# Ending two stages by token halves, with VectorE alone adding to x

## The reference

```python
y = memory_cross_attention(h, mem_n, w_mem_q, w_mem_kv, w_mem_o)  # ends in o @ w_mem_o, 1024 x 1024
x = x + rmsnorm(y, norm_mem_post)                                 # "mempost"
h = rmsnorm(x, norm_ffn_pre)                                      # "ffn"
y = conv_gated_ffn(h, w_up, ffn_dw, ffn_dw_b, w_down)             # ends in (...) @ w_down, 2816 x 1024
x = x + rmsnorm(y, norm_ffn_post)                                 # "ffnpost"
# the second network begins
h = rmsnorm_2(x, ffn1_norm[0])                                    # "f10"
x = x + 0.5 * ((silu(h @ w_gate) * (h @ w_up)) @ w_down)
```

## Time and profile before

| | |
|---|---|
| median of 3 executions | 2481.59 us (2478.96, 2481.59, 2482.19) |
| the profiled execution's own time | 2481.17 us |
| its span, first to last instruction | 2479.9 us |
| TensorE busy | 2444.1 us, 99% of the span |
| VectorE, ScalarE, GpSimd busy | 69%, 48%, 21% |
| chain that ended last | TensorE 86%, VectorE 8%, ScalarE 3% |
| mean granted TensorE clock | 0.994 of full speed |

### The profile page before, as it was taken

One profiled execution on the slowest core, in us unless ns is written; L12 is line 12 of the kernel. 1 busy time (PEld: TensorE's weight loads), 2 busy tenths in 40 slices (PEclk: granted clock), 3 DMA queues, 4 the chain that ended last, 5 costly groups with the idle time before them and its releaser, 6 DMA issues.

```text
span 2479.9 us, 36498 instructions
## 1 busy us (share of the span) xinstructions
PE 2444.1 (99%) x14390; PEld 2155.8 (87%) x14390; DVE 1709.8 (69%) x2772; ACT 1178.8 (48%) x2038; POOL 511.9 (21%) x441
## 2 busy tenths in 40 slices
PE   9999999999999999999999999999999999999999
PEld 7777777888887989898889898999998888899998
DVE  6896655556624868677868677767677666776766
ACT  4496443444423635355635355535354555554443
POOL 4772302122201201002201002010111432201010
PEclk9999999999999999999999999999999999999999
DMA  5212312333232656552646454555532111456563
GB/s 170 83 43 69 102 43 61 109 94 95 82 108 73 166 134 173 135 149 79 164 134 171 136 148 124 156 147 158 148 115 82 46 49 58 126 154 145 158 150 99
DMA packets 110299, 287.57 MB, mean 116 GB/s; under 512 B 12080, under 2 KB 13616, under 8 KB 110128
## 3 DMA queue, kind: packets, MB, share of 16 engines
q1 hardware_dynamic: 88240, 245.37, 31.5%
q0 software_dynamic: 21888, 39.86, 10.1%
HBM read 283.08 MB, written 2.10 MB: 115 GB/s over the span
## 4 chain that ended last, share of the span: by engine, by line
PE 86%; DVE 8%; ACT 3%; issue 2%; POOL 1%; DMA 0%; SPq 0%; ACTq 0%; POOLq 0%; DVEq 0%
PE main L602 10%; PE main L604 10%; PE main L603 10%; PE score L602 5%; PE score L604 5%; PE score L603 5%; PE main L2031 4%; PE main L2030 4%; PE main L2029 4%; PE score L2029 4%; PE score L2031 4%; PE score L2030 4%; PE out L2031 2%; PE out L2030 2%; PE out L2029 2%; PE out L602 2%
## 5 line engine op out<-in xcount | busy, mean ns | idle before, releaser
L553 DVE TENSOR_TENSOR wl<-raw,wh 128x512 fp32r<-128x512 f32 (+2 forms) x507 | 493.1, 977 | 257.7 <-ACT wh L544 253.0
L544 ACT ACTIVATE wh<-raw 128x512 fp32r<-128x512 f32 (+2 forms) x507 | 415.7, 837 | 474.6 <-PE main L604 242.7
L509 POOL DMA_DIRECT2D sum<-in_wts x152 | 132.9, 903 | 954.4 <-DMA sum<-in_wts 942.9
L553 DVE TENSOR_TENSOR wl<-sum,wh 128x512 fp32r<-128x512 f32 x304 | 207.3, 687 | 62.5 <-ACT wh L544 56.8
L602 PE MATMUL main<-hxh,wh 128*128 128x512 f32 x592 | 232.5, 393 | 2.2 <-DVE wl L553 1.6
L604 PE MATMUL main<-hxh,wl 128*128 128x512 f32 x592 | 230.7, 390 | 0.0
L603 PE MATMUL main<-hxl,wh 128*128 128x512 f32 x592 | 230.5, 389 | 0.0
L544 ACT ACTIVATE wh<-sum 128x512 fp32r<-128x512 f32 x304 | 177.3, 622 | 81.7 <-PE score L604 42.9
L689 POOL TENSOR_TENSOR acc<-acc,sq 128x512 f32<-128x512 f32 (+1 forms) x73 | 102.8, 1408 | 472.3 <-ACT sq L684 468.4
L2029 PE MATMUL score<-th,wh 128*128 128x256 f32 x548 | 155.4, 284 | 0.7 <-ACT kept L2133 0.5
L2030 PE MATMUL score<-tl,wh 128*128 128x256 f32 x548 | 155.1, 283 | 0.0
(11 more groups left out here) (549 smaller groups left out, 7142.8 us busy)
## 6 DMA issues: line engine op xcount, KB each, us to landing
raw<-in_wts SPq DMA_DIRECT2D x299, 512.0 KB, 3.6
sum<-in_wts SPq DMA_DIRECT2D x152, 256.0 KB, 3.1
sum<-in_wts POOLq DMA_DIRECT2D x152, 256.0 KB, 5.4
raw<-in_wts SPq DMA_DIRECT2D x80, 256.0 KB, 5.1
raw<-in_wts SPq DMA_DIRECT2D x52, 384.0 KB, 3.0
x<-in_xT SPq DMA_DIRECT2D x4, 512.0 KB, 7.8
out<-x SPq DMA_DIRECT2D x8, 256.0 KB, 2.0
memx<-in_memT SPq DMA_DIRECT2D x1, 1024.0 KB, 9.6
```

Of the source, the lines that this page charges most:

```text
L509: e.dma_start(t[:, :], stored(r + 1, part), accum_op=ALU.add).then_inc(*sig.up(("upper" if which == S3 else "gate") + f"_ended{n}", ("summ ...
L544: e.activation(halves_of(wh, i), src, ACT.Copy).then_inc(*sig.up("weight_high", ("high", i)))
L553: e.tensor_tensor(halves_of(wl, i), src, f(halves_of(wh, i)), ALU.subtract) \
```

## The change

`mempost` and `ffnpost` get an end of their own (`halved_end_*`); `mixpost` keeps the old one, only renamed (`mix_end_*`). Tokens 0 to 255 are half 0, tokens 256 to 511 half 1.

- **End of the product.** The last tiles (`SPLIT`: tiles 6 and 7 of the memory's product, tile 7 of the network's) are made first for half 0, then for half 1, with matmuls of 256 columns. Inside half 1 of the first of them TensorE sums the squares of half 0 and, four steps later, spreads its root. The squares of tiles 6 and 7 no longer go through GpSimd, and ScalarE copies the split tiles to SBUF.
- **Opening.** `halved_opening_tensor` takes three tiles instead of two: half 0 of tile 0 for k = 0 to 2, the sums of half 1, half 0 of tile 1 for k = 0 to 2, both for k = 3 to 7 (half 1's root is spread behind k = 5), half 0 of tile 2, then half 1 of all three, step by step with the new squares between.
- **Elementwise work.** Scaling, addition, `hxh`, square and `hxl` run on 256 tokens, first all 8 tiles of half 0, then all of half 1. All 16 additions to `x` stand on VectorE. GpSimd keeps one sum of two new squares (two in the stage `ffn`).
- **Weights.** `high` and `low` of the next stage's first three units stand among the steps of half 0.
- `keep_warm` is gone, and the order of PSUM banks changes (`wide.pass_over`, `FIRST_BANK`).

```diff
+        SPLIT = {"mempost": (6, 7), "ffnpost": (7,)}
+        def halved_opening_tensor(e, ended, nm, u, banks_of):
+            for n in range(2):
+                for k in range(3):
+                    opening_half(e, u + n, banks_of[n], nm, k, 0)
+                    opening_half_low(e, u + n, banks_of[n], nm, k, 0)
+                if n == 0:
+                    half_sums(e, ended, 1)
+            for k in range(3, KC):
+                for n in range(2):
+                    opening_half(e, u + n, banks_of[n], nm, k, 0)
+                for n in range(2):
+                    opening_half_low(e, u + n, banks_of[n], nm, k, 0)
+                if k == 5:
+                    half_rows(e, ended, 1)
+            for k in range(KC):
+                opening_half(e, u + 2, banks_of[2], nm, k, 0)
+                opening_half_low(e, u + 2, banks_of[2], nm, k, 0)
+            for k in range(KC):
+                for n in range(3):
+                    opening_half(e, u + n, banks_of[n], nm, k, 1)
+                for n in range(3):
+                    opening_half_low(e, u + n, banks_of[n], nm, k, 1)
+                if 1 <= k <= 4:
+                    squares_of(e, nm, k - 1)
+            squares_of(e, nm, 5)
+            if nm == "f10":
+                squares_of(e, nm, KC - 2)
+                squares_of(e, nm, KC - 1)
...
+        def halved_end_scalar(e, nm, u, parts, y, next_u, next_nm, gain):
...
+            for m in split:
+                half_kept_scalar(e, nm, u, parts, m, 0, y)
+            half_root_scalar(e, nm, 0)
...
+            if parts == 1:
+                half_kept_scalar(e, nm, u, parts, 6, 1, y)
+                high(e, next_u + 1)
+            else:
+                high(e, next_u)
+            for k in range(KC):
...
+                half_high_scalar(e, nm, read, next_nm, k, 0, gain)
+                if k == (1 if parts == 1 else 4):
+                    half_kept_scalar(e, nm, u, parts, KC - 1, 1, y)
+                if parts == 3 and k == 2:
+                    high(e, next_u + 1)
+                if k == (3 if parts == 1 else 5):
+                    half_root_scalar(e, nm, 1)
+                if k == (5 if parts == 1 else 7):
+                    high(e, next_u + 2)
+            for k in range(KC):
+                half_high_scalar(e, nm, ("unit", u + parts * KC - 1), next_nm, k, 1, gain)
...
+        def halved_end_vector(e, nm, u, parts, y, gain, next_u, next_nm, next_gain):
...
+            for h in range(2):
+                for m in range(KC + 1):
+                    if m < KC:
+                        half_normed_vector(e, nm, m, h, y, gain)
+                    if m < KC:
+                        half_added_vector(e, nm, m, h)
+                    if h == 0 and m == 1:
+                        low(e, next_u + (1 if parts == 1 else 0))
+                    if m > 0:
+                        half_low_vector(e, next_nm, m - 1, h, next_gain)
+                    if h == 0 and parts == 3 and m == 5:
+                        low(e, next_u + 1)
+                    if h == 0 and m == (6 if parts == 1 else 8):
+                        half_inverse_vector(e, nm, 1)
+                if h == 0:
+                    low(e, next_u + 2)
```

More of the change, by code:

```diff
@@ L1596, in build, with mix_end_tensor @@
         post_turn = Ring(tmp_slots)
[L1598 to L1601, removed]
+        def mix_end_tensor(e, nm, u, src, fillers):
+            b0, old = mainb.take(("y", nm, 0))
+            e.wait_ge(*sig.at(old))
+            b1, old = mainb.take(("y", nm, 1))
+            e.wait_ge(*sig.at(old))
+            for k in range(KC):
+                pair_step(e, u, b0[:, :], b1[:, :], src, k)
+            for m in range(2, KC):
@@ L1619, in post_product_tensor @@
[L1619 to L1640, removed]
+                linear(e, u + m, b[:, :], src)
+            mem_value_tensor(e, *fillers[0])
+            square_sums(e, nm, KC - 1)
+            mem_value_tensor(e, *fillers[1], rows=nm)
@@ L1666, in post_norm_vector @@
             inverse_vector(e, nm)
[L1667 to L1690, removed]
+            low(e, U_VAL[1][0] + 2)
+            low(e, U_VAL[1][1] + 2)
+            for m in range(KC + 2):
+                if m < KC:
+                    y_normed_vector(e, nm, m, y, gain)
+                if m > 1:
+                    split_low(e, next_nm, m - 2, next_gain)
+                if m < KC and m % 2 == 0:
+                    x_even_vector(e, nm, m)
+                if m in (2, 4):
+                    low(e, U_VAL[1][1 + m // 2] + 2)
+            mem_value_vector(e, 1)
         def y_normed_vector(e, nm, m, y, gain):
@@ new lines, in half_products @@
+        def half_products(e, nm, u, parts, m, p, h, src, ks):
+            i, b, c = u + parts * m + p, mainb.of(("y", nm, m, h)), HALF_OF[h]
+            wh_i, wl_i = weights_of(i)
+            last = units[i][2] - 1
+            e.wait_ge(*sig.at(("low", i)))
+            for k in ks:
+                sh, sl, ready = src(8 * p + k)
+                e.wait_ge(*sig.at(ready))
+                made = mm3(e, b[:, c], (wh_i[:, k, :], wl_i[:, k, :]), (sh[:, c], sl[:, c]), p == 0 and k == 0, p == parts - 1 and k == last)
+                if k == last:
+                    made.then_inc(*sig.up("unit_done", ("unit", i) if h else ("left", i)))
@@ new lines, in opening_half, with opening_half_low @@
+        def opening_half(e, i, o, nm, k, h):
+            w, lo = weights_of(i)
+            c = HALF_OF[h]
+            e.wait_ge(*sig.at(("low", i)))
+            e.wait_ge(*sig.at(("xhigh", nm, k, h)))
+            e.matmul(o[:, c], w[:, k, :], hxh[:, k, c], start=k == 0, stop=False)
+            e.matmul(o[:, c], lo[:, k, :], hxh[:, k, c], start=False, stop=False)
+        def opening_half_low(e, i, o, nm, k, h):
+            c = HALF_OF[h]
+            e.wait_ge(*sig.at(("split", nm, k, h)))
+            made = e.matmul(o[:, c], weights_of(i)[0][:, k, :], hxl[:, k, c], start=False, stop=k == KC - 1)
+            if h == 1 and k == KC - 1:
+                made.then_inc(*sig.up("unit_done", ("unit", i)))
@@ L2044, in opening_product @@
             u = U_OF[nm] + 2 * c
-            if which == UP and c == 0:
+            if (which == UP and c == 0) or (nm == "f10" and which == GATE and c == 1):
                 return
```

252 lines of the change are left out of this document (188 added, 64 removed).

## The result

Over 20 executions each the kernel before has a median of 2479.74 us (2477.93 to 2485.53) and the changed one 2483.12 us (2481.74 to 2486.39). The ratio is 1.0014, 95% interval [1.0007, 1.002]: 3.4 us slower. The forecast was 2480.0, 1.6 us faster than the median of three shown ahead of it (2481.59, itself 1.85 us above the median of twenty). The change is inside the 0.2% that was called no change, but it goes the other way.

What follows compares the result with a forecast made beforehand. TensorE, busy 99% of the span, was taken as the bound. Terms of -1.9 (memory), -0.8 (network) and +1.0 (block f10) made -1.7 us on 2481.17; with the median 0.4 higher, 2479.9, said as 2480, range 2474 to 2485.5.

Steps and rivals of the forecast that it cites:

- Gain 1.9 us: Memory's end: the fourth tile and a last group of squares end at 439.3 us against 441.2 before.
- B: Theory of the follow-up experiments, not the prediction: one of the two halved ends is slow by itself, whatever the clock does.
- a matter of position: Clock at memory's end before: granted 0.57 from 420 to 428, 3.4 us lost; the network's similar instructions had no fall.
- rival 2: Clock falls in the new stalls at both ends: one fall 2483.4 us, two 2486.8; chance 0.16, one fall 0.09.
- VectorE per tile and half: Openings: scaling, addition and `hxl` on 256 columns take VectorE 1.25 us per tile.
- third and fourth tile, memory, t: Memory's end: tile starts at 13.8 and 31.4 us, counted from the start of half 0's spread rows.
- network's stage: Network's end and f10's opening: the fourth tile begins at 814.5 against 815.30, a gain of 0.8 us.
- start of block f10: Behind the network's opening: ScalarE's copies for the turned sums come later, costing 1 us, bounds 0 and 4.
- stalls of the first half: Openings, half 0: TensorE waits for VectorE 2.9 us at the memory's end and 2.5 at the network's.
- stretched `hxl`: Openings: with GpSimd's additions gone, no `hxl` instruction on VectorE would be stretched.
- Rival 1: VectorE keeps up, so the first-half stalls of 2.9 and 2.5 us vanish: 2473.6 us; chance 0.24.
- Rival 3: Fourth unit and turned sums come later than counted, 2 us more at each place: 2484 us; chance 0.08.

Runs made afterwards that it cites:

- odd_gpsimd: Changed kernel with odd tiles' additions to `x` moved back to GpSimd, by halves, at both ends: 2482.79 us, ratio 1.0014 to the kernel before.
- after_look: Changed kernel, nothing altered, profiled a second time: 2482.17 us.
- net_only: Only the network's end and f10's opening halved, memory's end as in the kernel before, with its fillers: 2482.18 us, ratio 1.001.
- fill_stalls: Changed kernel with matmuls that nobody reads put into TensorE's waits at both ends: 2481.11 us, ratio 1.0 to the kernel before.
- after: First profile of the changed kernel, nothing altered: its profiled execution took 2482.98 us.
- net_no_filler: Network's end and f10's opening halved, memory's end as in the kernel before but without its fillers: 2481.02 us, ratio 1.0002.
- Mem_no_filler: Memory's end halved, network's end as in the kernel before but without its fillers: 2480.72 us, ratio 1.0003.

## Why the prediction was wrong

**The step that failed is the base: "Gain 1.9 us" at the memory's end.** It set a new end without a fall against the old one's 441.2, which held a fall of 3.4 us lost. The working of the new end was right: the stage was to take 87.30 - 1.9 = 85.4 us and took 85.57. That it came out as a gain of 1.73 us in the pair of profiles was luck: the one execution of before had a fall there and the one of the changed kernel had none. Undisturbed against undisturbed it is 85.6 against 84.4 us, a loss of 1.2 us by the halving itself, so much of B is true. TensorE stands idle for 3.50 us of the halved stage and for 2.01 us of the old one, and what the old opening does not have is the wait of 1.44 us for the fourth unit's weights. The text saw the fall, called it "a matter of position", and then neither took it out of the base nor put one into the forecast. Set against 84.43 us, its own 85.4 is a loss of 1 us.

**The clock, rival 2.** The forecast's sum had no fall; the rival priced one at 2483.4, nearly the measured 2483.1, and had 0.09 for it. So near a hit is luck: it starts from a gain that was not there and from a median of three. In 7 of the 8 profiles with a halved network's end the clock falls in its stage, so this should have been the main case. Of the seven where the two waits around the sums of half 1 stand unfilled (1.07 and 1.06 us, in odd_gpsimd 1.39 and 1.09), five fall at the second wait or within 0.5 us behind it; with fillers in them that fall was gone and another came at 814. The Trainium skill, "TensorE: Matmul & The Clock Gate", section "HAM oscillation — how this bites in real kernels", tells of pauses between groups of matmuls that bring the lower clock. Its case has pauses of several microseconds; here two of about one, with one-column matmuls between, went ahead of a fall in five of seven profiles, so it agrees in kind, not in every execution. What the rival did not have is that the old ends fall too, and that without fillers this costs them some 0.4 us.

**Other terms.**

| term | forecast | measured |
|---|---|---|
| VectorE per tile and half | 1.25 us | 1.25 us |
| third and fourth tile, memory, t | 13.8, 31.4 | 13.8, 31.4 |
| wait for the fourth unit, memory | 1.5 us | 1.44 us |
| third and fourth tile, network, t | 15.2, 33.0 | 17.5, 35.2 with a fall; 15.9, 33.7 without (odd_gpsimd) |
| network's stage | -0.8 us | +3.11 us; 0.0 without a fall |
| start of block f10 | +1.0 us | +1.44 us; 0 to 3.1 us in the other profiles with this order |
| stalls of the first half | 2.9 and 2.5 us | 2.06 and 2.13 us |
| stretched `hxl` | none | one at each end, 1.51 and 1.50 us, waited for by nobody |

The network's term is the second that failed: 0.8 us of it was not there even undisturbed, and with falls the stage took 3.1 us more. The start of the block was well bounded (0 to 4). In the changed kernel's profile no wait there was longer than 1 us (0.47, 0.23 and 0.80). How late it is goes with the fall ahead of it: with 3.4 us lost between 811 and 823 (after_look, net_only, fill_stalls) the block takes 0 to 0.2 us more than before, with 1.7 us lost there (after, net_no_filler) 1.44 and 1.82, with none (odd_gpsimd) 3.05, of which a fall inside it is a part. A fall there seems to hide the wait for VectorE, so the 0.0 of the network's stage is not that end's whole price.

Rival 1 fell: VectorE kept the pace counted, and TensorE waited, though 0.8 and 0.4 us less than counted; at the network it waited for ScalarE's square and for weights, not for `hxl`. Rival 3's first place, the fourth unit, was no later than counted; its second, the block, was so in some profiles.

**What stays open.** A profile is one execution, and the falls change places between executions. Mem_no_filler's executions run from 2476.69 to 2483.31 us, and its profile is of the slowest (it lost 3.4 us at 1150 to 1160 too, where nothing was changed). Of the 4.3 and 4.6 us that one halved end costs, 2.9 are found in the changed stretches; where the rest lies is not settled, nor how the 2.9 divide between falls and the longer stages. More clock lost is not all of it: among executions of the same mean granted clock, 0.994, the old ends without fillers took 2476.4 to 2478.3 us (5 of them), net_no_filler 2478.7 to 2481.2 (6) and mem_no_filler 2480.0 to 2481.9 (6). What makes the clock fall in one execution and not in the next is not shown. Nor was it tried to give the opening's fourth unit a buffer of its own, which might take the wait of 1.44 us away, or to test the new order of PSUM banks alone.

## What to carry to other kernels

Before a difference is counted against a profile, take out of the base what only that execution had: a stage with a slow clock in it is not the stage. The price of a fall is its place: where TensorE waits for another engine anyway it cost next to nothing here, and fillers that only put it off moved it to where it cost most of itself. So time the kernel without its fillers before tuning around them.

## What was not expected of the hardware

- A fall that costs next to nothing: in the opening a step takes 2.70 us at 1.2 GHz and at 2.4 GHz alike, and the kernel before is 0.15% faster without its twice 6 fillers, although its clock falls at both ends.
- GpSimd holds VectorE up without an addition to `x`. In the changed kernel `hxl` at 429.12 and at 804.48 takes 1.51 and 1.50 us, each beside GpSimd's sum of two squares (for the first the timeline of GpSimd below); the first ends 0.3 us behind that sum's end at 430.35. The prediction had put the long `hxl` down to the additions. In the profile of before 13 of the 25 that take over 0.9 us overlap a sum of squares and no addition. The Trainium skill, "SBUF — State Buffer", section "SBUF: two separate sides", says that the two share a pair of ports, which one holds for a whole instruction; these two instructions agree.

```profile
428.95 1.40 POOL L690 TENSOR_TENSOR sq<-sq,sq 128x512 f32<-128x512 f32 x1 [28.89 <-ACT sq L1824]
```
